# Entering the expert projection in eight pieces, with the first weight units split ahead

## What is computed

```
h2 = rmsnorm(x) * gain (+ shift, in the first block)
q  = h2 @ w_q                                    # 1024 x 2048: the "projection"
s  = einsum('thpd,hpnd->thpn', q, sub_keys)      # the "scores"
idx, g = top_k over the product of the two halves, softmax
act = gelu(einsum('thkd,td->thk', u_tab[idx], h2))
x  += einsum('thk,thkd->td', g * act, v_tab[idx])
```

## Time and profile before

| | |
|---|---|
| time, median of 3 runs | 2532.55 us (2528.1 to 2536.94) |
| the profiled execution's own time | 2529.04 us |
| its span | 2527.1 us |
| mean granted TensorE clock | 0.973 of full |
| busy: PE, PEld | 2357.0 us, 2098.7 us |
| busy: DVE, ACT, POOL | 1620.4 us, 1216.9 us, 424.0 us |

### The profile page before, as it was taken

The page is one execution under the profiler, slowest core; times in us unless marked ns, Lnnn a source line. Parts: engine busy times, 40 slices in busy tenths (PEclk is TensorE's granted clock), DMA queues, the critical chain, the costliest instruction groups (busy, mean ns, idle before and its releaser), DMA issues.

```text
span 2527.1 us, 47068 instructions
## 1 busy us (share of the span) xinstructions
PE 2357.0 (93%) x14990; PEld 2098.7 (83%) x14990; DVE 1620.4 (64%) x3524; ACT 1216.9 (48%) x2578; POOL 424.0 (17%) x262
## 2 busy tenths in 40 slices
PE   7989979999997899999799899989999997899998
PEld 2767779999996788888668677779999996788887
DVE  2465345887877777777215674345887878777776
ACT  1356135555557555555223522035555557555554
POOL 0000000267763000000000000000277673000000
PEclk9989989999999999999899899989999999999999
DMA  6566443577762466665243322444577672466664
GB/s 234 175 225 217 158 150 141 183 183 183 182 184 55 155 210 206 211 209 203 102 142 117 100 89 96 142 153 147 183 181 181 185 180 52 159 214 211 211 214 166
DMA packets 190936, 422.57 MB, mean 167 GB/s; under 512 B 54256, under 2 KB 89328, under 8 KB 190208
## 3 DMA queue, kind: packets, MB, share of 16 engines
q1 hardware_dynamic: 149824, 413.73, 48.2%
q0 software_dynamic: 36864, 0.15, 4.3%
q10 hardware_dynamic: 4160, 7.64, 0.9%
HBM read 403.48 MB, written 17.96 MB: 167 GB/s over the span
## 4 chain that ended last, share of the span: by engine, by line
PE 87%; DVE 7%; issue 3%; ACT 2%; ACTq 0%; DMA 0%; DVEq 0%; PEld 0%; PEldq 0%
PE ps L714 20%; PE ps L1321 19%; PE ps L1315 11%; PE ps L1316 11%; PE ps L1317 11%; PE ps L1322 10%; PE ps L796 2%; DVE arena L1598 1%; DVE gbuf L1564 1%; PE ps L1007 1%; PE ps L985 1%; PE ps L1589 1%; PE ps L1353 1%; DVE gbuf L808 0%; PE ps L999 0%
## 5 line engine op out<-in xcount | busy, mean ns | idle before, releaser
L1321 PE MATMUL ps<-csplit,hl 128*128 128x512 f32 x2048 | 720.9, 397 | 7.0 <-DVE hl L1638 7.0
L1532 POOL DMA_INDIRECT gates<-gbuf,picks_at x256 | 423.2, 1653 | 1686.5 <-DVEq L1501 1517.3
L1315 PE MATMUL ps<-hsplit,hl 128*128 128x256 f32 x2304 | 656.6, 285 | 31.8 <-DVE hl L1393 31.8
L1316 PE MATMUL ps<-hsplit,hl 128*128 128x256 f32 x2304 | 655.7, 285 | 0.0
L1317 PE MATMUL ps<-hsplit,hl 128*128 128x256 f32 x2304 | 655.6, 285 | 0.0
L1322 PE MATMUL ps<-csplit,hl 128*128 128x256 f32 x2048 | 576.3, 281 | 0.0
L1393 DVE TENSOR_TENSOR hl<-ring,hl 128x512 fp32r<-128x512 f32 x576 | 399.1, 694 | 236.7 <-ACT hl L1390 225.7
L1390 ACT CAST hl<-ring 128x512 fp32r<-128x512 f32 x576 | 355.3, 620 | 371.6 <-PE ps L1317 370.9
L1315 PEld LDWEIGHTS ps<-hsplit,hl 128*128 128x128 f32 x2304 | 446.2, 194 | 32.9 <-ACT hl L1390 32.9
L1321 PEld LDWEIGHTS ps<-csplit,hl 128*128 128x128 f32 x2048 | 385.9, 188 | 97.8 <-issue 7.3
L714 PE MATMUL ps<-arena,ring 128*128 128x256 f32 (+2 forms) x1896 | 444.8, 394 | 15.5 <-issue 10.8
(11 more groups left out here) (196 smaller groups left out, 1830.4 us busy)
## 6 DMA issues: line engine op xcount, KB each, us to landing
ring<-stream SPq DMA_DIRECT2D x723, 512.0 KB
gates<-zeros SPq DMA_DIRECT2D x32, 512.0 KB, 5.0
gring<-gates SPq DMA_DIRECT2D x256, 64.0 KB, 2.9
gates<-gbuf,picks_at POOLq DMA_INDIRECT x256
arena<-keys ACTq DMA_DIRECT2D x2, 1024.0 KB, 4.9
gbuf<-consts ACTq DMA_DIRECT2D x1, 1120.0 KB, 5.0
arena<-xT ACTq DMA_DIRECT2D x1, 1024.0 KB, 10.6
arena<-ctxT ACTq DMA_DIRECT2D x1, 1024.0 KB, 12.9
```

The costliest lines, as they stand in the source:

```text
L1315: pe.matmul(out_ap, w[0], m[0], start=start, stop=False)
L1316: pe.matmul(out_ap, w[1], m[0], start=False, stop=False)
L1321: pe.matmul(ps[:, bank, :], w_hi, m_both, start=start, stop=False)
L1532: pool.indirect_dma_start(out=cells, out_offset=bass.IndirectOffsetOnAxis(ap=picks_at[:, i, c:c + 1], axis=0), in_=gates[:, i, c:c + 1], i ...
```

## The change

1. TensorE gives three places of `hl` back before the last eight tiles (a drain). ACT splits the first three halves of the projection weights before its last two squares (`before_square`), DVE their low parts around the last tile.
2. h2 enters in eight pieces. DVE alternates between the product of one group and the low part of the group two before (`enter_peer`); ACT makes the high parts one by one (`enter_act`), in block 1 with the shift in the same instruction, so that L868 goes away. TensorE's first unit waits for one group at a time. The fourth half is split behind the pieces.
3. The first four halves (two units) of table u are split by ACT and DVE around the last projection takes, ahead of the score copies. TensorE's first four units of u wait for one bank's copy each.
4. `rs1` and `pt1` move in SBUF, out of the way of the early halves. The key load of block 2 is issued before the entry and not behind `peer_in`.

```diff
-    probs1, pt1 = G1.take(2, 512), G1.take(2, 512)
+    probs1 = G1.take(2, 512)
+    silu_c = G1.take(KD, 2)
+    G1.at = 3 * 2 * HALF
     rs1 = G1.take(2, 512)
+    pt1 = G1.take(2, 512)
     cprod = G1.take(2, T)
-    silu_c = G1.take(KD, 2)
...
+    EARLY = 3
+
+    def early_hi(act, b, half, table="wq"):
+
+        unit, h = units[f"{table}{b}"][0] + half // 2, halves(b, table) + half
+        if half % 2 == 0:
+            act.wait_ge(S(arrival(unit)[0]), arrival(unit)[1])
+        act.wait_ge(S("split_used"), h + HLRING * (b - 1) + 1)
+        act.copy(hl[:, h % HLRING, 0, :], slot(unit)[:, half % 2 * HALF:(half % 2 + 1) * HALF])\
+           .then_inc(S("split_hi"), 1)
+
+    def early_lo(dve, b, half, table="wq"):
+
+        unit, h = units[f"{table}{b}"][0] + half // 2, halves(b, table) + half
+        dve.wait_ge(S("split_hi"), h + 1)
+        dve.tensor_tensor(hl[:, h % HLRING, 1, :], slot(unit)[:, half % 2 * HALF:(half % 2 + 1) * HALF],
+                          hl[:, h % HLRING, 0, :].bitcast(F32), ALU.subtract).then_inc(S("split_lo"), 1)
+
+    def before_square(b):
+        def f(act, k):
+            if k == KD - 2:
+                early_hi(act, b, 0)
+                early_hi(act, b, 1)
+            if k == KD - 1:
+                early_hi(act, b, 2)
+        return f
+
+    ENTER_LAG = 2
+
+    def enter_peer(b, gain):
+
+        def f(dve, root):
+            for k in range(KD + ENTER_LAG):
+                if k < KD:
+                    dve.scalar_tensor_tensor(h_full[:, k, :], resid[:, k, :], gain(k), root, ALU.mult, ALU.mult)\
+                       .then_inc(S("peer_in"), 1)
+                j = k - ENTER_LAG
+                if j < 0:
+                    continue
+                dve.wait_ge(S("hsplit_hi"), (b - 1) * KD + j + 1)
+                hi, lo = hsplit[:, 0, j, :].bitcast(F32), hsplit[:, 1, j, :]
+                if b == 1:
+                    ins = dve.scalar_tensor_tensor(lo, h_full[:, j, :], mod[:, 24 + j, 0:1], hi, ALU.add, ALU.subtract)
+                else:
+                    ins = dve.tensor_tensor(lo, h_full[:, j, :], hi, ALU.subtract)
+                ins.then_inc(S("hsplit_ready"), 1)
+        return f
+
+    def enter_act(act, b):
+
         for k in range(KD):
-            ins = eng.scalar_tensor_tensor(h_full[:, k, :], resid[:, k, :], scale2[:, k:k + 1], root, ALU.mult, ALU.mult)
-        chain(ins, eng)
-        for k in range(KD):
-            ins = eng.tensor_scalar(h_full[:, k, :], h_full[:, k, :], mod[:, 24 + k, 0:1], None, ALU.add)
-        ins.then_inc(S("peer_in"), 1)
+            act.wait_ge(S("peer_in"), (b - 1) * KD + k + 1)
+            if b == 1:
+                ins = act.activation(hsplit[:, 0, k, :], h_full[:, k, :], ACT.Identity, bias=mod[:, 24 + k, 0:1])
+            else:
+                ins = act.copy(hsplit[:, 0, k, :], h_full[:, k, :])
+            ins.then_inc(S("hsplit_hi"), 1)
...
+                    if first:
+                        eng.wait_ge(S("hsplit_ready"), (b - 1) * KD + k + 1)
                     w = [hl[:, hslot, x, n * P:(n + 1) * P] for x in range(2)]
                     m = [hsplit[:, x, k, :] for x in range(2)]
                     mm = passes(eng, ps[:, s % 4, 0:T], w, m, k == 0, k == KD - 1)
                 mm.then_inc(S("split_used"), 1)
-            if kind == "act":
+            if kind == "act" and 2 * s + half >= ready:
...
+            if kind == "dve" and 2 * s + half >= ready:
                 eng.wait_ge(S("split_hi"), i * 2 * per + (h0 + half + 1))
                 eng.tensor_tensor(hl[:, hslot, 1, :], raw, hl[:, hslot, 0, :].bitcast(F32), ALU.subtract)\
                    .then_inc(S("split_lo"), 1)
-                if extra:
-                    extra(2 * s + half)
+            if kind == "dve" and extra:
+                extra(2 * s + half)
...
-        pe.wait_ge(S("peer_in"), b)
-        pe.drain().then_inc(S("split_used"), HLRING)
-        pe.wait_ge(S("hsplit_ready"), b)
-        u_loop("pe", pe, b, 0, NQ // UB, table="wq")
+        u_unit("pe", pe, b, 0, 0, first=True, table="wq")
+        pe.wait_ge(S("peer_in"), KD * b)
+        pe.drain().then_inc(S("split_used"), HLRING - EARLY)
+        for s in range(1, UB):
+            u_unit("pe", pe, b, 0, s, table="wq")
+        u_loop("pe", pe, b, 1, NQ // UB, table="wq")
         peer_pe_scores(pe, b)
-        pe.wait_ge(S("peer_s_copied"), 8 * b)
-        u_loop("pe", pe, b, 0, TURN_UNIT // UB)
+        for s in range(UB):
+            pe.wait_ge(S("peer_s_copied"), 8 * (b - 1) + 5 + s)
+            u_unit("pe", pe, b, 0, s)
+        u_loop("pe", pe, b, 1, TURN_UNIT // UB)
...
-        act.wait_ge(S("peer_in"), b)
-        act.copy(hsplit[:, 0, :, :], h_full).then_inc(S("hsplit_hi"), 1)
         act.drain().then_inc(S("u_bank_free"), 4)
+        enter_act(act, b)
         for s in range(UB):
-            u_unit("act", act, b, 0, s, first=True, table="wq")
+            u_unit("act", act, b, 0, s, first=True, table="wq", ready=EARLY)
         u_loop("act", act, b, 1, NQ // UB, table="wq")
+        early_hi(act, b, 0, "u")
+        early_hi(act, b, 1, "u")
         take_unit(act, b, NQ // UB, -2, table="wq")
+        early_hi(act, b, 2, "u")
         take_unit(act, b, NQ // UB, -1, table="wq")
+        early_hi(act, b, 3, "u")
...
+            u_unit("act", act, b, 0, s, first=True, ready=HLRING)
...
-        dve.wait_ge(S("hsplit_hi"), b)
-        dve.tensor_tensor(hsplit[:, 1, :, :], h_full, hsplit[:, 0, :, :].bitcast(F32), ALU.subtract)\
-           .then_inc(S("hsplit_ready"), 1)
-        u_loop("dve", dve, b, 0, NQ // UB, table="wq")
+        for s in range(UB):
+            u_unit("dve", dve, b, 0, s, table="wq", ready=EARLY)
+        u_loop("dve", dve, b, 1, NQ // UB, table="wq")
+        for half in range(HLRING):
+            early_lo(dve, b, half, "u")
...
+            u_unit("dve", dve, b, 0, s, extra=between, ready=HLRING)
...
-            act.wait_ge(S("peer_in"), 2)
             act.dma_start(keys_area, keys2).then_inc(S("keys_loaded2"), 16)
...
-            take_tiles("dve", dve, group_of["out1"])
+            take_tiles("dve", dve, group_of["out1"][:-1])
+            early_lo(dve, 1, 0)
+            early_lo(dve, 1, 1)
+            take_tiles("dve", dve, group_of["out1"][-1:])
+            early_lo(dve, 1, 2)
...
-            pe_tiles(pe, group_of["out1"])
+            pe_tiles(pe, group_of["out1"][:-KD])
+            pe.drain().then_inc(S("split_used"), EARLY)
+            pe_tiles(pe, group_of["out1"][-KD:])
...
-            for g in ("wo_gla", "w_out"):
-                pe_tiles(pe, group_of[g])
+            pe_tiles(pe, group_of["wo_gla"])
+            pe.drain().then_inc(S("split_used"), EARLY)
+            pe_tiles(pe, group_of["w_out"])
```

More of the change, by code:

```diff
@@ L748, in __init__ @@
         def __init__(self, src, squares, n, cols, groups, lhs, width, root, ready, gain, dst=None, done=None, apply=None, fill=None,
-                     each=None, done_each=None):
+                     each=None, done_each=None, before_square=None):
+            self.before_square = before_square
             self.fill = fill
@@ L899, in build @@
     norm_ffn = Norm(resid[:, :, :], sq2, KD, T, [list(range(KD))], ones, D, rs2, [],
-                    lambda k: v_("norm_ffn", k), dst=lambda k: h_full[:, k, :], done="peer_in",
+                    None, apply=enter_peer(2, lambda k: v_("norm_ffn", k)), before_square=before_square(2),
                     each=lambda k: ("taken_dve", ffn_taken - KD + k + 1))
@@ L1363, in peer_act_scores, with u_unit @@
                      ps[:, (4 if t == 0 else 0) + n, :]).then_inc(S("peer_s_copied"), 1)
-    def u_unit(kind, eng, b, i, s, per=4, extra=None, first=False, table="u"):
+    def u_unit(kind, eng, b, i, s, per=4, extra=None, first=False, table="u", ready=0):
         unit = units[f"{table}{b}"][0] + s
@@ L1698, in peer_act @@
         for s in range(P):
-            u_unit("act", act, b, 0, s, first=True)
+            u_unit("act", act, b, 0, s, first=True, ready=HLRING)
             if s in exp_at:
@@ L1728, in peer_dve @@
         for s in range(P):
-            u_unit("dve", dve, b, 0, s, extra=between)
+            u_unit("dve", dve, b, 0, s, extra=between, ready=HLRING)
         for g in range(HOT_AHEAD):
@@ L1931, in _ @@
             take_tiles("dve", dve, group_of["wo_mla"][6:])
-            for g in ("wo_gla", "w_out"):
-                take_tiles("dve", dve, group_of[g])
+            take_tiles("dve", dve, group_of["wo_gla"])
+            take_tiles("dve", dve, group_of["w_out"][:-1])
+            early_lo(dve, 2, 0)
+            early_lo(dve, 2, 1)
+            take_tiles("dve", dve, group_of["w_out"][-1:])
+            early_lo(dve, 2, 2)
             norm_ffn.dve(dve)
```

7 lines of the change are left out of this document (3 added, 4 removed).

## The result

The changed kernel took 2503.87 us (median of 6 runs, 2498.38 to 2508.97), the kernel before, on the same chip in turn with it, 2533.45 (6 runs, 2525.41 to 2536.94). The ratio is 0.9887, with an interval of 0.9866 to 0.9909: 28.6 us less (23 to 34). It is faster by 1.1%, and the interval leaves out a ratio of 1. The time lies at the lower edge of the range.

What follows compares the result with a forecast made beforehand. TensorE bounds the kernel, so time is won where it stands still or runs at the lower clock. Gains of 6.1 (first entry), 4.2 (second) and 10.0 (scores) sum to 20.3: 2532.55 - 20.3 = 2512.2, forecast 2512, range 2503 to 2523.

Steps and rivals of the forecast that it cites:

- A: The forecast as worked out, terms at bad to good ends: 14.5 to 24.7 us gained, 2507.5 to 2518; chance 0.65.
- the four waits: TensorE's waits for low weight parts, 31.8 us at two entries and two scores; what leaves them should leave the time.
- First pass of each entry: At the two entries, TensorE's wait before its first pass falls to 4.5 and 4.4 us.
- DVE's sixteen instructions: At each entry, eight products and eight low parts in turn, 0.43 us each at the first, 0.42 at the second.
- TensorE has done the unit 0.7 us later: At each entry, TensorE keeps up group by group and ends its first unit 0.7 us after the last low part.
- The clock behind the unit: At each entry, the low clock lasts 4.6 us from unbroken feeding, partly behind the first unit, losing 1.7 us.
- Drains: Two new TensorE drains, ahead of the last eight tiles and behind the unit, cost 0.25 us each, 0.5 per entry.
- Early splits hidden: Ahead of the entry, early weight splits of 0.55 to 0.69 us each fit into idle times of 3.0, all hidden.
- Scores, 5.0 each: At the end of each scores, TensorE goes straight on: 3.5 us of gap and 1.5 of low clock come back.
- Rival B: The clock does not come back: 0.5 us more at each entry, 1.5 at each score; time 2516; chance 0.20.
- Rival C: Early splits ahead of the entries come late if loads land slowly: gain 9.1 us, time 2523; chance 0.10.
- Rival D: TensorE's four written-out stretches of passes bring issue waits costing 52 us: time 2564, slower; chance 0.05.

Runs made afterwards that it cites:

- e1: The changed kernel with its score part undone, so the entries alone: 2515.57 us, ratio 0.9931 to the kernel before.
- e2: The kernel before with the score part of the change alone, entries untouched: 2520.36 us, ratio 0.9943 to the kernel before.
- e6: The changed kernel without the early splits of table u, banks still waited for one by one: 2516.8 us, run once.
- e9: The changed kernel with ten matmuls of no use on TensorE behind the last sum of squares at each entry: 2510.05 us, run once.
- e4: The changed kernel with h2 split whole, as before, but the projection weights still split early: 2519.98 us, ratio 0.9949 to the kernel before.

## Why the prediction was right, and where its sum was off

The forecast was 2512 with faster at 0.88; it came to 2503.87. By the stages the sum of 20.3 should have been 24.5, close to 24.7, where all terms stand at their good ends. That the time lies inside the stated range is luck: 28.6 us lies outside A's own range of 14.5 to 24.7, and inside the stated range only because that was widened by 4.5 for the spread of runs. (A's lower end, 2507.5, should read 2532.55 - 24.7 = 2507.9.)

- **What bounds it, and that what leaves the four waits leaves the time:** right. The waits fell by 22.7 us, the stages by 24.5, and e1 and e2 add up.
- **First pass of each entry** at 4.5 and 4.4 us behind the sum: 4.62 and 4.49.
- **DVE's sixteen instructions**, 0.43 and 0.42 each: they took 350.06 - 343.64 = 6.42 us, 0.40 each, and 1654.50 - 1648.56 = 5.94, 0.37 each. The last low part came 0.5 and 0.8 us sooner than worked out.
- **"TensorE has done the unit 0.7 us later":** 1.3 us and 1.2, since it ran at the low clock and three low parts came in quick succession at the end. About 0.5 against me at each entry.
- **The clock behind the unit (4.6 us from when TensorE is fed without a break, so 1.7 lost):** this is the step that failed, a term of the sum that was mis-sized. The clock rose 5.5 us (first entry) and about 4.6 (second, the first pass of 0.28 at 1654.90) after the first pass, though the first groups came with pauses between them: its rise stood in both cases within the unit, and nothing was lost behind it. The end that I had named, "nothing, if it counts from the first piece", was the case. The first entry gave 7.9 against 6.1, 1.8 more, the second 6.3 against 4.2, 2.1 more. This term is 1.7 of each; DVE adds 0.5 and 0.8, the unit's end takes about 0.5, and 0.25 comes from the first drain, which costs nothing that these stages hold. That closes to within 0.2.
- **Drains** at 0.25: the one behind the unit shows as 0.26 of issue at both entries. The one ahead of the last eight tiles shows no cost: TensorE stands idle for 1.02 us there with and without it, and from there to the last sum of squares it takes 30.9 us in both kernels, at both entries (301.43 to 332.36 before, 309.51 to 340.45 after).
- **Early splits hidden:** right. The squares stay 3.45 apart (331.03, 334.48, 337.94), and the late sum of this run (340.5) is not theirs: e1 has the same early splits and its last sum at 333.8, e2 has none and 333.5.
- **Scores, 5.0 each:** 5.3 and 5.1. The gap of 3.5 went, and the clock stayed at 1.00. The 1.5 of this for the clock was read from one execution of the kernel before; e1 and e6 show 0 and 2.4 for the same gap, so that it came out this well is in part chance. The cover of the fifth half, 1.9, was 1.6 and held.
- **Rival B** (the clock does not come back) fell: the passes at 0.64 us of each 0.79 did bring it back. The Trainium skill, TensorE: Matmul & The Clock Gate, section HAM oscillation, tells of waits for a load, each longer than the burst before it, behind which every burst starts at the low level. The prediction took this for its case, and the page's rule does not bear on it: the groups followed each other at 0.72 to 0.87 us, so the pauses behind their 0.64 were 0.1 to 0.2 us and far shorter than the bursts. Over such pauses the level rose, and in e9, with waits of 0.2 to 0.3 us between groups, it held.
- **Rival C** (late early splits) did not come: first casts at 331.35, in the idle time between two squares. **Rival D** (code) did not come: 22.1 us of issue in 11 waits against 22.6 in 14, none before the new passes but the drain's 0.26 twice.

The timed difference, 28.6, is 4 above the stages, within its interval; the timed differences of e1 to e4 also stand 1 to 5 above theirs (17.5 against 15.2, 14.4 against 10.5, 21.3 against 16.1, 12.9 against 12.2). Each is within its interval. That they lean to one side is not explained, but it is less than it seems: e1 to e4 share one set of fifteen runs of the kernel before, and by the medians their differences are 15.8, 11.1, 19.4 and 11.4. The untouched entries of e2 agree with those of before to 0.1 us; what the rest is stays open.

## What to carry to other kernels

Where the engine that bounds the kernel waits at the end of a chain of whole-tensor steps, cutting the operand into pieces pays only together with whatever else stands between the last step and that engine: here the pieces alone gave 5.7, the early weight splits alone 1.8, both 14.1. Before judging one of two such edits, ask of the trace what the engine would wait for next. A gap on TensorE costs its length and then, if the clock falls, the low clock until it rises again: a wait of 3.6 us at the scores cost 3.8 where the clock held, 5.1 to 5.3 in the kernel before, and 6.2 where it stayed low longest. But where something slower feeds TensorE anyway the low clock is nearly free: keeping TensorE busy ahead of the entry bought 0.4 us at one entry and nothing that could be shown at the other.
